# Hybrid attention and MoE decoder step: the row fetch of the next item moves to between the second and third pair of weights

## The reference

```
logits = x2d @ w_router + b_router            # 32 experts, top 4 of them per token
gates  = softmax(top_vals)
# for each expert e and the rows routed to it:
gu  = xb @ w_gate_up[e] + b_gate_up[e]        # 1024 -> 2 x 1024
g   = minimum(gu[:, :1024], 7);  u = clip(gu[:, 1024:], -7, 7)
hid = (u + 1) * (g * sigmoid(1.702 * g))
out = hid @ w_down[e] + b_down[e]             # 1024 -> 1024
y[token] += gate * out
x = layer_norm(deepnorm_alpha * x + y, ln2_g, ln2_b)
```

## Time and profile before

| what | value |
|---|---|
| time, median of 3 runs (lowest to highest) | 1326.35 us (1326.22 to 1326.98) |
| the profiled execution's own time | 1327.01 us |
| its span | 1325.2 us |
| TensorE matmuls busy | 1271.4 us (96%) |
| VectorE, ScalarE, GpSimd busy | 457.1, 260.4, 85.5 us |
| HBM read over the span | 493.58 MB, 375 GB/s over the span with the writes |
| L1815 gate and up matmuls, x2112 | 462.2 us busy |
| L1863 down matmuls, x1056 | 233.9 us busy |
| L1461 row fetch, x408 | 95.1 us busy |
| chain that ended last | PE 50%, DMA 23%, ACT 2%, DVE 1% |

### The profile page before, as it was taken

One profiled execution on the slowest core, in us unless ns is written; L12 is line 12 of the kernel. 1 busy time (PEld: TensorE's weight loads), 2 busy tenths in 40 slices (PEclk: granted clock), 3 DMA queues, 4 the chain that ended last, 5 costly groups with the idle time before them and its releaser, 6 DMA issues.

```text
span 1325.2 us, 19517 instructions
## 1 busy us (share of the span) xinstructions
PE 1271.4 (96%) x7682; PEld 514.0 (39%) x7683; DVE 457.1 (34%) x986; ACT 260.4 (20%) x607; POOL 85.5 (6%) x92
## 2 busy tenths in 40 slices
PE   8999997999999999999999999999999999999995
PEld 6354444664433333333333333333333333333332
DVE  1265364775842232222332222233222232222225
ACT  1333345753420110100110100011100110100002
POOL 2023234310010000000000000000000000000000
PEclk9999998999899999999999999999999999999998
DMA  9679779887589999999999995999999999999992
GB/s 367 243 292 355 253 312 372 303 357 256 199 313 409 426 429 428 428 428 427 430 429 428 428 428 234 406 426 428 430 428 428 428 429 428 428 430 429 427 428 93
DMA packets 53308, 498.38 MB, mean 376 GB/s; under 512 B 6793, under 2 KB 7945, under 8 KB 26386
## 3 DMA queue, kind: packets, MB, share of 16 engines
q1 hardware_dynamic: 41586, 430.62, 77.9%
q0 software_dynamic: 11520, 67.11, 13.1%
q10 hardware_dynamic: 160, 0.07, 0.0%
HBM read 493.58 MB, written 3.93 MB: 375 GB/s over the span
## 4 chain that ended last, share of the span: by engine, by line
PE 50%; DMA 23%; ACT 2%; DVE 1%; issue 0%; SPq 0%; ACTq 0%; DVEq 0%
PE psum L1815 25%; DMA arena<-in_w_gate_up 23%; PE psum L1863 11%; PE psum L1461 4%; PE psum L1796 3%; PE psum L1644 2%; PE psum L1476 2%; PE psum L1469 1%; ACT arena L1945 1%; ACT arena L1979 1%; PE psum L1628 1%; PE psum L1667 0%; PE psum L1656 0%; DVE arena L2353 0%; PE psum L1639 0%
## 5 line engine op out<-in xcount | busy, mean ns | idle before, releaser
L1815 PE MATMUL psum<-arena 128*64 128x512 f32 x2112 | 462.2, 593 | 11.5 <-DMA arena<-in_w_gate_up 11.5
L1815 PEld LDWEIGHTS psum<-arena 128*64 128x64 f32 x2112 | 150.4, 137 | 316.0 <-issue 288.4
L1863 PE MATMUL psum<-arena 128*64 128x512 f32 x1056 | 233.9, 595 | 3.3
L2296 DVE TENSOR_SCALAR arena<-psum 128x512 f32<-128x512 f32 x33 | 22.8, 692 | 610.6 <-PE psum L1815 610.6
L1863 PEld LDWEIGHTS psum<-arena 128*64 128x64 f32 x1056 | 72.9, 137 | 150.2 <-issue 131.9
L2243 DVE SCALAR_TENSOR_TENSOR arena<-psum,arena 128x1024 f32<-128x1024 f32 (+1 forms) x96 | 103.3, 1103 | 69.4 <-PE psum L1800 37.2
L1975 ACT ACTIVATE arena<-arena 128x512 f32<-128x512 f32 x32 | 20.2, 630 | 455.4 <-DVE arena L2296 455.4
L1461 PE MATMUL psum<-arena 128*64 128x512 f32 x408 | 95.1, 601 | 0.0
L1191 DVE STREAM_TRANSPOSE arena<-arena 128x1024 f32<-128x1024 f32 x64 | 75.0, 1217 | 1.8 <-DVE arena L1291 0.9
L1796 PE MATMUL psum<-arena 64*128 64x512 f32 x264 | 65.9, 615 | 1.9 <-issue 1.9
L1983 ACT ACTIVATE arena<-psum 128x512 f32<-128x512 f32 x33 | 19.7, 597 | 239.8 <-PE psum L1863 239.8
(11 more groups left out here) (268 smaller groups left out, 1001.0 us busy)
## 6 DMA issues: line engine op xcount, KB each, us to landing
arena<-in_w_gate_up SPq DMA_DIRECT2D x128, 2048.0 KB, 19.6
arena<-in_w_down SPq DMA_DIRECT2D x62, 2048.0 KB, 16.6
arena<-in_w_in SPq DMA_DIRECT2D x12, 1024.0 KB, 11.8
arena<-in_w_out SPq DMA_DIRECT2D x4, 1024.0 KB, 10.6
arena<-in_w_down SPq DMA_DIRECT2D x4, 1024.0 KB, 13.9
arena<-in_x_prompt SPq DMA_DIRECT2D x4, 512.0 KB, 5.0
out<-arena SPq DMA_DIRECT2D x8, 256.0 KB, 6.3
arena<-in_ln_g SPq DMA_DIRECT2D x2, 512.0 KB, 7.6
```

Source lines behind the costliest of these rows:

```text
L1815: ins = nc.tensor.matmul(psum[64 * h:64 * h + 64, n, :], x_k, slot[k][:, col:col + 512], start=False, stop=(k == KD - 1))
L1863: ins = nc.tensor.matmul(psum[64 * h:64 * h + 64, 7, :], h_k, slot[s][:, col:col + 512], start=(k == 0), stop=(k == KD - 1))
```

## The change

The call of `fetch(t + 1)` in TensorE's body moves for all items but the first. It stood behind all eight k steps of the gate and up products; it now stands in the k loop, behind k = 3, so behind the second pair of weights (pair 2) and its `w_used`, and ahead of the wait for the third (pair 4). Nothing else changes: not the matmuls of the fetch, not VectorE's, ScalarE's or SyncE's programs.

```
                         if k == 6 and first:
                             tables()
-                    fetch(t + 1)
+                        if k == 3 and not first:
+                            fetch(t + 1)
                     if first:
+                        fetch(t + 1)
                         turn_gates()
                     else:
                         pe.wait_ge(y_copied, t)
```

## The result

The changed kernel takes 1332.68 us (median of 6 runs, 1331.74 to 1335.38), the kernel before 1326.45 in the same comparison (1325.84 to 1328.44). The ratio is 1.0049, with a 95% interval of 1.0036 to 1.0062: slower by 6.2 us. The forecast was 1332.8 us. The profiled execution has a span of 1331.1 us and a time of its own of 1332.87; amounts of work are the same, 19517 instructions.

The account below looks back on a forecast made before the run. Weight loads were taken to bound the kernel, TensorE 1.23 us per item behind; 32 waits of 0.65 us less 14.34 us of vanished weight waits give +6.5, so 1326.35 becomes 1332.8 us, range 1324.5 to 1338.5.

Parts of the forecast that it names:

- TensorE was second by little: Weight loads pace items at 29.41 us against TensorE's 28.18, 1.23 apart; TensorE's waits for weights total 14.34 us.
- The fetch costs 2.57 us anywhere in the loop, with no switch and no wait: The 12 fetch records move from behind pair 6 to ahead of pair 4, taking 2.57 us without waiting.
- The cover: The fetch behind the gate and up products hid VectorE's block 0 drain; without it TensorE waits before the hidden transposes.
- Its size: New TensorE wait for the block 0 drain: net 0.58 to 0.70 us per item, 0.65 taken.
- X: Start of what follows the gate and up products; hidden transposes, ready at X + 3.51, were forecast to go at X + 4.21.
- the restart: Hidden transposes' matmuls, 0.12 us behind their weight load before, would start with it after a wait, partly offsetting 0.70.
- The sum: Over 32 items, 20.8 us of new waiting, of which 14.34 replaces waits for weights: +6.5 us.
- the loads stay the bound: Rival: VectorE's drain not in the way, fetch falls into TensorE's waits for weights; 1321.2 to 1323.9 us, chance 0.12.
- The wait near the break-even: Rival: wait for the drain between 0.33 and 0.53 us per item, 1323.9 to 1329.0 us, no change; chance 0.13.
- The dear switches: Rival: fetch between two pairs also costs 0.11 us per side for shape switches, 0.87 per item, 1339.9 us; chance 0.10.
- The overlap of 0.08 between VectorE instructions: VectorE's next independent instruction starts 0.61 us after one lasting 0.69; without this overlap the wait is 0.73, time 1335.4.
- `w_used` of pair 4: Release of pair 4's weight slot comes 2.57 us later against pair 2's; no cost was given to it.

Follow-up runs that it names:

- e5: Kernel before, with half of pair 10 of w_down not loaded for experts 2 to 31: 1313.02 us, ratio 0.9892.
- e4: Changed kernel with the fetch behind the third pair of weights (k = 5) instead of the second: 1334.2 us, ratio 1.0054.
- e1: Changed kernel, TensorE's wait for the block 0 drain moved behind the hidden transposes, row transposes and ScalarE's copies reordered: 1323.15 us, ratio 0.9978.
- e2: Kernel before, fetch in its old place, with the same reordering of wait, transposes and copies as e1: 1326.47 us, ratio 0.9998.
- e8: Changed kernel plus one unread 128x256 VectorE copy per item ahead of the drain of block 0: 1341.15 us, ratio 1.0108.
- e7: Kernel before plus one unread 128x256 VectorE copy per item ahead of the drain of block 0: 1326.53 us, ratio 0.9997.
- e6: Changed kernel, with half of pair 10 of w_down not loaded for experts 2 to 31: 1334.22 us, ratio 1.0061.
- e3: Changed kernel, scatters of blocks 1 and 2 before the hidden transposes, block 0 after, drains in order 2, 1, 0: 1326.03 us, ratio 1.0002.
- e9: Changed kernel with the late wait of e1 and the fetch behind the third pair (k = 5): 1324.54 us, ratio 0.998.

## Why the prediction was right

*TensorE was second by little.* Right: the loads bound, and TensorE was 1.2 us per item behind. e5 shows the 14.34 us of waits for weights to the hundredth (901.78 against 32 x 28.18 = 901.76).

*The fetch costs 2.57 us anywhere in the loop, with no switch and no wait.* Right. In the changed kernel the gate and up products start again 2.58 us behind the fetch's start (481.84 to 484.42 in the item after the one shown), and e4 gives the same item stage at another place.

*The cover.* Right. The wait in front of the hidden transposes is there, 32 times, released by the drain; e1 takes the wait out of the way and keeps the fetch's place, and what the move costs per item falls from 0.69 us to 0.29; e2 makes the same edit where the drain was covered, and the time stays (0.12 us per item, which e1 has too, is the reordering's own); e8 and e7 do the same with a longer way to the drain.

*Its size.* The wait is 0.69 us per item, 0.65 was forecast. The chain of starts came out within 0.01 us of the working up to the hidden transposes (X + 4.20 against 4.21). The 0.04 lies in what I let the restart win back: the group's matmuls start with their weight load, as said, but it also lasts 0.74 us, and the two nearly cancel. The net was 0.69 to 0.70, the upper of my two values.

*The sum.* With 0.69 it is 32 x 0.69 - 14.34 = +7.7 against a forecast of +6.5; the item stage grew by 7.76. The medians grew by 6.23, so the forecast of the median, 0.1 us off, is closer than its own terms are. That is luck: the time ahead of item 1 alone differs by 2.27 us between the two profiled executions.

*The rivals.* That the loads stay the bound fell with the twelve pieces that left the chain, and with e6. It is also the case that the rule of the most contended resource, of the Trainium skill's Perfetto Trace Analysis (section Identifying the Most-Contended Engine), would have backed: DMA was that resource, and giving it nothing more to do while TensorE's order changed made the kernel slower. The wait near the break-even did not occur, though e3 built it and landed on 1326. The dear switches did not occur. The overlap of 0.08 between VectorE instructions held: the drain starts 0.61 behind the product's start, for a length of 0.69. The Trainium skill's VectorE: DVE Perf Modes (section The DRAIN you can't avoid) says that the next instruction doesn't start until the pipe has emptied, but goes on that one which isn't held starts earlier; the prediction left out the second half, and it is the one that these starts agree with.

What the prediction lacked is the load side of such a move when TensorE's period is short again. I wrote that `w_used` of pair 4 comes 2.57 us later and gave it no price. In the changed kernel it has none. In e1 the account, which has this term at nothing, was short by 3.8 us in the item stage of one execution and by 1.5 in the medians. The traces show some 1.0 us of loads that came later behind the doubled expert; the rest of the shortfall stays open.

## What to carry to other kernels

Before work is moved away from a place, list what finished under its cover there: an instruction that waits for nothing in the old trace may be next in line for a wait that was always met in time. The price is read from starts and durations (here an engine's chain of five instructions against TensorE's), and then compared with the slack between the bound and the engine that is second, since new waiting first eats that. Where a cover has gone, moving the wait behind work that doesn't need it (e1) can give more than the move cost.

## Of the hardware, not expected

The time ahead of item 1 differs between executions of programs that are the same there, 386.99 to 392.27 us over twelve, while the TensorE-paced items repeat to the hundredth (28.18, 28.35 and 28.87 us). In e9's profile 2.08 us without work on TensorE were followed by matmuls at a granted clock of 0.51. And a VectorE copy of 128x256 that lasts 0.29 us moves the start of what follows it by 0.20 only.
